# Ten early up-projection blocks in place of eight, four of them set beside another stage, and one weight load moved behind three small ones

## The reference, cut to what matters

```python
def block_fn(args):                       # PEER, 128 tokens at a time
    tb, ib, gb = args
    u = u_tab[ib]
    act = gelu(einsum("td,thkd->thk", tb, u))
    vv = v_tab[ib]
    return einsum("thk,thkd->td", (gb * act), vv)

def _conv_ffn(h, w_up, conv_w, conv_b, w_down):   # D_FF = 2816, w_up (1024, 5632)
    u = h @ w_up
    up = jnp.pad(u, ((0, 0), (1, 1), (0, 0)))
    u = up[:, :-2] * conv_w[0] + up[:, 1:-1] * conv_w[1] + up[:, 2:] * conv_w[2] + conv_b
    a, v = jnp.split(u, 2, axis=-1)
    return (jax.nn.silu(a) * v) @ w_down
```

## Time and profile before

| | |
|---|---|
| time, median of 3 runs | 1709.84 us (1707.72 to 1710.06) |
| profiled execution, its own time | 1709.84 us |
| its span | 1708.0 us, so 1.84 us lie around it |
| TensorE, VectorE, ScalarE, GpSimd busy | 1483.1, 1041.2, 526.5, 744.5 us |
| moved by DMA | 487.40 MB, of it 268.47 MB by the gathers' queue |
| first gather to last landing | about 312 to 1218 us |

### The profile page before, as it was taken

The page is one execution under the profiler, slowest core; times in us unless marked ns, Lnnn a source line. Parts: engine busy times, 40 slices in busy tenths (PEclk is TensorE's granted clock), DMA queues, the critical chain, the costliest instruction groups (busy, mean ns, idle before and its releaser), DMA issues.

```text
span 1708.0 us, 22384 instructions
## 1 busy us (share of the span) xinstructions
PE 1483.1 (87%) x8446; PEld 1041.2 (61%) x8446; DVE 1041.2 (61%) x2200; ACT 526.5 (31%) x833; POOL 744.5 (44%) x676
## 2 busy tenths in 40 slices
PE   9999999827576777766899999998699999999999
PEld 8997675724121323323755555555399986699997
DVE  5864534897597858778756764411244146568865
ACT  6743331211022111213322220002233064466652
POOL 0035310577777867776636454553100023026750
PEclk9999999968788888887999999999799999999999
DMA  7448851799999999999999997986668757545551
GB/s 275 149 148 336 311 204 38 281 377 343 401 390 397 366 391 405 394 406 357 402 380 331 345 364 294 379 292 238 222 202 291 271 203 291 198 141 172 181 196 52
DMA packets 160267, 487.40 MB, mean 285 GB/s; under 512 B 10144, under 2 KB 13984, under 8 KB 156960
## 3 DMA queue, kind: packets, MB, share of 16 engines
q0 software_dynamic: 73728, 268.47, 41.1%
q1 hardware_dynamic: 86432, 217.51, 34.9%
HBM read 484.89 MB, written 1.05 MB: 285 GB/s over the span
## 4 chain that ended last, share of the span: by engine, by line
PE 45%; DMA 2%; DVE 2%; issue 1%; ACT 1%; POOL 0%; ACTq 0%; DVEq 0%; POOLq 0%
PE ps L761 44%; DMA wring<-in_ups 1%; DMA arena<-in_peer_v,cl 1%; PE ps L765 1%; DMA wring<-in_attn_w_qkv 0%; ACT arena L2439 0%; DVE st L2345 0%; POOL arena L3096 0%; DVE pr L1645 0%; ACT wh L2442 0%; ACT sqb L2439 0%; DVE prT L2362 0%; DVE cbase L1648 0%; ACT xT L2439 0%; DVE qT L1642 0%
## 5 line engine op out<-in xcount | busy, mean ns | idle before, releaser
L761 PE MATMUL ps<-arena,wring 128*32 128x512 f32 (+6 forms) x2984 | 714.5, 473 | 121.5 <-DMA arena<-in_peer_v,cl 100.3
L761 PEld LDWEIGHTS ps<-arena,wring 128*128 128x128 f32 (+1 forms) x2984 | 398.6, 173 | 420.4 <-DMA arena<-in_peer_v,cl 168.5
L3096 POOL DMA_INDIRECT arena<-in_peer_u,arena x214 | 248.1, 1159 | 261.6 <-PE ps L761 131.1
L2028 DVE CUSTOM_DVE_ANT_0 arena<-arena 128x1024 f32<-128x1024 f32 x214 | 256.7, 1224 | 122.2 <-DMA arena<-in_peer_u,arena 119.0
L3096 POOL DMA_INDIRECT arena<-in_peer_v,cl x214 | 228.2, 1066 | 111.2 <-issue 60.0
L2439 ACT ACT_TABLE_LOAD x68 | 87.2, 1283 | 348.8 <-DVE arena L2028 206.4
L1648 DVE SCALAR_TENSOR_TENSOR cvs<-ps,vec,cvs 128x255 f32<-128x255 f32 (+3 forms) x236 | 104.4, 443 | 73.3 <-ACT cvs L2439 66.1
L761 PE MATMUL ps<-hhl,wh 128*128 128x256 f32 (+1 forms) x528 | 126.2, 322 | 0.6 <-POOL hhl L3106 0.4
L761 PEld LDWEIGHTS ps<-arena 128*128 128x128 f32 (+1 forms) x708 | 86.7, 194 | 46.8 <-issue 28.3
L1642 DVE TENSOR_TENSOR wl<-wring,wh 128x2048 fp32r<-128x2048 f32 (+1 forms) x42 | 92.2, 2195 | 36.8 <-ACT wh L2442 35.9
L761 PE MATMUL ps<-arena 128*128 128x128 f32 (+4 forms) x708 | 98.5, 291 | 18.3 <-DVE arena L1645 6.5
(11 more groups left out here) (279 smaller groups left out, 2206.8 us busy)
## 6 DMA issues: line engine op xcount, KB each, us to landing
wring<-in_ups SPq DMA_DIRECT2D x37, 2048.0 KB, 9.5
wring<-in_ada SPq DMA_DIRECT2D x24, 2048.0 KB, 9.6
wring<-in_ffn_w_down SPq DMA_DIRECT2D x12, 2048.0 KB, 7.8
wring<-in_w_in SPq DMA_DIRECT2D x8, 2048.0 KB, 8.3
wring<-in_ffn_w_down SPq DMA_DIRECT2D x6, 1536.0 KB, 7.3
wring<-in_peer_wq SPq DMA_DIRECT2D x4, 2048.0 KB, 16.1
wring<-in_attn_w_qkv SPq DMA_DIRECT2D x4, 2048.0 KB, 8.4
wring<-in_w_out SPq DMA_DIRECT2D x2, 2048.0 KB, 11.1
```

The source lines that it names most:

```text
L761: return pe.matmul(o, l, r, start=start, stop=stop)
L2028: ve.tensor_tensor_reduce(out=o, in0=o, in1=h2[:, t, :], scale=1.0, scalar=0.0, op0=MUL, op1=ADD, accum_out=dots[j % 2][:, k:k + 1]).then_ ...
L3096: po.indirect_dma_start(out=ring[n % NR], out_offset=None, in_=table, in_offset=bass.IndirectOffsetOnAxis(ap=which, axis=0)).then_inc(S[f" ...
```

## The change

Ten blocks are visited early in place of eight, and four of the ten ctx visits are done behind steps 0, 1, 8 and 9 of `first_half`. The other six stand 20 rests apart. The places behind them are spaced anew: `first_half`'s steps 1.2 rests apart (1.9 before), the a visits 2.3 (2.1), the both visits 6.4 (5.8), the gap behind them 2 times 1.5 (1), the down pieces 3.2 and 2.4 (2.9 and 2.2). The load "kvc" goes behind the three small loads. With EARLY_BLOCKS the number of ("cup", "ctx", g) loads goes from 4 to 5, that of a visits from 8 to 10, that of both visits from 14 to 12; the eleven ("cup", "both", g) stay.

```diff
-    EARLY_BLOCKS, BESIDE = 8, ()
+    EARLY_BLOCKS, BESIDE = 10, (0, 1, 8, 9)
...
         for f in range(BEFORE_A + 2):
             places.append(n)
-            n += 15 if f < BEFORE_A else 2
+            n += 20 if f < BEFORE_A else 2
         n = max(n, 311)
-        for lengths in ([1.9] * 14, [2.1] * EARLY_BLOCKS, [5.8] * (22 - EARLY_BLOCKS), [1] * 2,
-                        ([2.9] * 8 + [2.2] * 4) * 2, [1] * 11):
+        for lengths in ([1.2] * 14, [2.3] * EARLY_BLOCKS, [6.4] * (22 - EARLY_BLOCKS), [1.5] * 2,
+                        ([3.2] * 8 + [2.4] * 4) * 2, [1] * 11):
...
-        load("kvc", ("p_ckv", 3), kcols(a["attn_w_qkv_2"][0], 1024, 512), n=3)
         sp.wait_ge(*at("p_cd", 24))
         sp.dma_start(cl[:, 0:512], a["c_late"][:, 0:512]).then_inc(S["d_l"], 16)
         sp.dma_start(hpC[:, 0:1568], a["c_bands"]).then_inc(S["d_l"], 16)
         sp.dma_start(nfb, a["normf_g"].partition_broadcast(128)).then_inc(S["d_g2"], 16)
+        load("kvc", ("p_ckv", 3), kcols(a["attn_w_qkv_2"][0], 1024, 512), n=3)
         nth[0] = 0
         sp.wait_ge(*at("p_v", 248))
         load("pool", ("p_pl", 4), pool_w(), n=3)
```

## The result

The changed kernel takes 1719.05 us (median of 4 runs, 1716.17 to 1722.26), the kernel before, with a fourth run added, 1709.95 us (1707.72 to 1712.17). The ratio is 1.0053, with a 95% interval of 1.0031 to 1.0076: half a per cent slower, where 0.5% faster was forecast. The profiled execution of the changed kernel took 1717.76 us, with a span of 1715.9.

What follows compares the result with a forecast made beforehand. DMA bound the kernel up to about 815 us, TensorE from 855 on. Terms -5.4 + 19.6 - 21.2 + 0.9 - 4 + 2 = -8.1 us took 1709.84 to 1701.7 us; range 1693 to 1710, with rivals 1716.

Steps and rivals of the forecast that it cites:

- part 1: Before rest 311: one weight tile less, 2.10 MB, in a stretch full of DMA at 391 GB/s, -5.4 us.
- part 2: Rest 311 to the first both visit: with added ctx and a visits, 104 us where 84.4 were, +19.6.
- part 5: Near the end: the kvc load moved behind the small loads lands later, +2 us; bounds 0 and 11 us late.
- signs of being wrong: DMA under 362 GB/s with share 1.0 in both visits, or over 112 us from rest 311 to first both visit.
- the wide stretch: The stretch of the both visits, in which TensorE was forecast to need 362 GB/s from DMA.
- the 104 us: Forecast time from rest 311 to the first both visit: 90.3 us of work plus two waits of 7 us.
- Part 3: Two both visits less at 10.6 us each, -21.2 us, and +0.9 for `v` rows that come there.
- part 4: The 5.38 us wait at 1028.28, before the down pieces, should go: -4 us taken, bounds 0 to -5.4.
- equal turns: Reading by which a tile alone on its queue needs at most 10.5 us and 104 becomes 98; the prediction rejected it.
- the wide stretch did not become DMA's: Rival: DMA can't give 362 GB/s, so bytes count to 1028 us; +7.4 us, 1717.2 us, chance 0.18.
- The a visits waited for tiles: Rival: a visits bound by tiles, one in 12.7 us, both 5 landing 12 us later; 1713.7 us, chance 0.15.
- their stretch moved 375 GB/s: Rival: the a visits' stretch moves only 355 GB/s, 104 becomes 112 us; 1709.4 us, chance 0.1.

Runs made afterwards that it cites:

- e1: Changed kernel with the kvc load back in its old place, ahead of the wait for the down-projection; ratio 1.0011 to the kernel before.
- e2: Kernel before with only the kvc load moved behind the three small loads; ratio 1.0052 to the kernel before.
- e3: Changed kernel with the kvc load behind the wait for the down-projection but ahead of the three small loads; ratio 1.0029.
- e4: Kernel before with ten early blocks, all ctx visits ahead of rest 311, none beside, both visits 6.3 rests apart, kvc in its old place; ratio 0.9940.
- e5: e4 with four ctx visits beside steps 0, 1, 8 and 9, the other six 20 rests apart; ratio 1.0000 to the kernel before.
- e6: e4 with the change's spacings behind rest 311, none beside; ratio 0.9917 to the kernel before.
- e7: e4 with two ctx visits beside steps 0 and 1, the other eight 15 rests apart; ratio 0.9953 to the kernel before.
- e8: e4 with two ctx visits beside steps 8 and 9, the other eight 15 rests apart; ratio 0.9978 to the kernel before.
- e9: e4 with only half of each of the a visits' five weight tiles fetched, output not the reference's; ratio 0.9885 to the kernel before.
- e10: Kernel before (eight blocks, none beside) with the change's spacings, both visits 5.9 rests apart; ratio 0.9968.

## Why the prediction was wrong

By the spans the change came out 16.0 us worse than forecast (+7.9 against -8.1). Of these, 1.7 lie in part 1, 3.0 in part 2, 5.8 in parts 3 and 4, 5.3 in part 5 and 0.2 behind it. Neither of the two things that were named as signs of being wrong came: DMA moved 377 GB/s in the wide stretch, and the 104 us became 107.0. The steps that failed are the load's move and "the wait should go".

**Part 5 (kvc) failed most.** It had bounds of 0 and 11 us and took +2, "DMA has share 0.61 here". The 0.61 is a mean over 1158 to 1196. In the trace of the kernel before, the part of that window in which the tile has to come is full:

```profile
1158.10:1173.60 15.50, 7.41 (x49) 3.73 (x48) 7.08 (x14) 7.73 (x11) 7.54 (x8) 0.93 0.96 360
1173.60:1193.80 20.20, 20.15 (x96) 16.03 (x96) 0.04 (x1) 1.37 (x3) 3.76 (x4) 0.88 0.41 144
```

DMA's idle time lies behind the moment at which kvc is wanted. TensorE works on the ctx keys then and uses no `v` row, so GpSimd has no free buffer to fetch into:

```profile
1185.20 0.94 POOL L3096 DMA_INDIRECT arena<-in_peer_v,cl  x1 [13.48 <-PE ps L761]
```

The tile took not 2.10/0.401 us behind the small loads but

```profile
wring<-in_attn_w_qkv SPq DMA_DIRECT2D x1, 2048.0 KB, 24.7
arena<-in_c_bands SPq DMA_DIRECT2D x1, 784.0 KB, 8.9
arena<-in_normf_g SPq DMA_DIRECT2D x1, 512.0 KB, 11.1
```

so that TensorE waited 10.7 us more, near the pessimistic bound, which stood on the 25.4 us of the earlier trace rows. Between the end of the down pieces and the last `v` row 7.3 us of that stay against the kernel before, and 9.2 against e1, which differs from the changed kernel in nothing else (68.9 and 59.7); in e2 4.8 stay. In time, e2 alone is +0.52%, and taking the move out of the change gives 1.0053 - 1.0011 = 0.42%, across two sets. DMA engines begin a queue's transfers in order: the Trainium skill says so of each engine's ring ("DMA: Bandwidth & Descriptors", queues, rings and completion order), and e3 agrees, with 7 us less once the tile was first.

Part 2 had said that equal turns between the queues do not hold, since they would bring a tile in 10.5 us and one took 17.1. That was a wrong reading. The same section of the Trainium skill has the engines take turns by packets, and this case's traces agree. Equal turns are then equal numbers of packets, not of bytes. From 833 to 852 us of the kernel before, with tiles and gathers both under way, the gathers' queue and SyncE's moved nearly the same number of packets (the numbers are packets, MB, share):

```profile
q0 software_dynamic: 1339, 4.84, 64.8%
q1 hardware_dynamic: 1360, 2.74, 38.2%
```

A gather's packets are 3.6 KB in the mean and a tile's 2.0, so the tile's queue gets 36% of the bytes, 144 of 401 GB/s. A tile alone in its queue then needs 14.6 us, an estimate from these rows; 16 to 19 were measured. By the same share the 3.69 MB that SyncE's queue has at kvc's place need 25.7 us, so that the tile would have been forecast some 9 us later than at 1175.6.

**Parts 3 and 4, -24.3, measured -18.5.** Part 3 was right: TensorE is busy for 149.60 + 128.34 = 277.9 us where it was 298.0, 20.1 less, and 20.3 were forecast. What failed is part 4, "the wait should go". The 5.38 us wait for VectorE's pick did go, but one of 5.81 for the weights' turn came in its place, since VectorE still has the last both visit's taps and product in front of it:

```profile
1025.59 0.55 DVE L1642 TENSOR_TENSOR cl<-cbase 128x376 f32<-128x376 f32 x1 [3.69 <-ACT cbase L2439]
...
1028.66 0.28 DVE L1648 SCALAR_TENSOR_TENSOR wt<-arena 128x64 f32<-128x64 f32 x1
```

With another of 1.16 at 1092.2 the waits are 7.0 us where they were 5.4: +1.6 in place of -4, which is nearly all of the 5.8 us. In the other kernels with ten blocks the twelve both visits take 143 to 147 us until the first down piece, about 12.1 each, and a wait of 4.4 to 5.8 us for VectorE stands behind them in every one.

**Part 2, +19.6, measured +22.6,** was near in its sum: TensorE is busy for 41.62 + 0.01 + 46.62 = 88.3 us (90.3 forecast) and waits for 18.7 (14 forecast). The a visits started 54.1 us behind rest 311 (55 forecast), the first both visit 107.0 (104). Its two tile waits, 2.80 and 3.48, were 6.3 us of the 7 put on them, and the wait before the a visits was 10.3 rather than 7. That it came so near is in part luck: e1 and e3, with the same work there, take 111.8 and 108.6 us, and the idle time before the a visits was ended by ScalarE, not by a weight tile as forecast. In the full table of the stretch this step is nevertheless where the change loses most against what ten blocks can bring: e4's 97.9 us from rest 311 to the first both visit became 114.1 in e5. The prediction had both numbers that say so, the slack of TensorE before rest 311 and the 28.8 us of added work behind it, and compared only with the kernel before. It did not ask what the same change is worth without the part that moves work from a stretch with slack into one that is on the path.

**Part 1, -5.4, measured -3.7** by the absolute time. By the stretch it is smaller than forecast. SyncE's queue moved 8.14 MB between the 166th gather and rest 311 in the kernel before and 6.05 in the changed one, one tile less as forecast, and 10.24 in e4 and e6. The four kernels with 6.05 MB (after, e1, e3, e5) take 196.9 us on average, the six with 8.14 (before, e2, e7, e8, e9, e10) 199.3, the two with 10.24 202.7. That is about 2.9 us for a tile, half of the 5.4 that its bytes would take at 391 GB/s; in the kernels with 6.05 MB the gathers moved about 1 MB more in this time. TensorE's work counts for nothing there: e9, with 158.8 us of it before rest 311, is no slower than e10 with 148.5. No run tells why a tile costs only half.

**The range** of 1693 to 1710 (1716 with the rivals) did not follow from the parts. Its upper end is the forecast and part 2's +8; the upper bounds of parts 1, 4 and 5, 5.4, 4 and 9 us more, were named and not counted. All together they reach 1728, and the measured 1719 lies inside that.

Of the rivals, the wide stretch did not become DMA's (377 GB/s in the changed kernel, with one TensorE wait in it, for VectorE). The a visits waited for tiles, but for 6 us rather than the 12 added ones of that rival, and their stretch moved 375 GB/s. None of the rivals had kvc as the thing that decides, though its own bound of 11 us was enough to turn the sum to +0.9.

What stays open: the first pair's own cost (e7 against e4 is 0.13%, inside the intervals), why the ratio of e3 is 0.2% above e1's when their profiles differ by less, and twelve early blocks, which were not run.

## What to carry to other kernels

When a load is moved later, read the DMA share of exactly the time in which it must come, not of a window that reaches past the point where it is wanted: here the mean held an idle time that came only behind that point. And before work is put "beside" a chain to fill an engine's waits, compare with the place it leaves: where that has slack, as here under a full DMA, moving the work out frees nothing by itself, and each engine's share of the moved work (`mid` and `taps` here) stands in the chain's way as well. Try the parts of a bundled change one by one: here the ten blocks were worth -0.6 to -0.8%, and two other parts took it back.

## What the runs showed of the hardware

A 2 MB tile takes 9.4 us when the gathers stand still (issued at 781.49 in the changed kernel, while TensorE held the ring), 16 to 19 as the only tile beside them, 25.4 in a row of three, and 24.7 behind 1.6 MB of its own queue:

```profile
wring<-in_ups SPq DMA_DIRECT2D x1, 2048.0 KB, 9.4
```

With both queues full, they moved the same number of packets (1339 and 1360), and so bytes in the ratio of their packet sizes. With TensorE's waits filled, its granted clock was 1.00 in the 45 us behind rest 311, where it had been 0.75. The 166th gather was issued between 570.9 and 583.7 us in twelve executions with the same work until there.
